# Gate rows written through DRAM by transfers, and half a gate tile ahead of the second attention pass's scores

## The chip, the core and the metric

The kernel runs on one core of one Trainium2 chip, as one launch. The metric is the time of one execution on the device in microseconds (us). It is the median of several runs; one more execution is profiled.

## The reference

Two transformer blocks in float32 over 256 tokens of width 1024. Cut to what matters here:

```
# first block
mod = silu(c) @ w_ada + b_ada;  shift_m, scale_m, gate_m, shift_f, scale_f, gate_f = split(mod, 6)
p = modulate(rms_norm(x), shift_m, scale_m) @ w_in
y_a = rwkv7_mix(p...)                 # recurrence over 12 heads, group norm, gate, @ w_a
y_b = dilated_attention_mix(p...)     # 12 heads in 3 groups, windows and dilations, @ w_b
x = x + gate_m * rms_norm((sigmoid(p_ga) * y_a + sigmoid(p_gb) * y_b) @ w_out)
x = x + gate_f * rms_norm(swiglu(modulate(rms_norm(x), shift_f, scale_f)))
# second block, for l in 0, 1
mod = (silu(c_2) @ w_ada[l] + b_ada[l]).reshape(3, 3, 1024)
x = x + 0.5 * mod[0, 2] * swiglu(ada_norm(x, 0))
x = x + mod[1, 2] * token_mixer(ada_norm(x, 1))
x = x + 0.5 * mod[2, 2] * swiglu(ada_norm(x, 2))
return rms_norm(x) * final_g
```

Every gate (`gate_m`, `gate_f`, `mod[., 2]`) is one number per column of the width, the same for all tokens. So is `final_g`.

## The kernel before

One program per engine, written out by hand. The engines meet at semaphores. Every transfer is issued by SP, in the order of its program, and SP does each wait in that order too.

**How a gate row comes about.** The modulation is computed by VectorE as dot products, one output per partition, so a gate lies as a column: `mod_gate` is [128, 8], the width spread over partitions and 8 columns. The hand-over at the end of a stage needs it as a row, [128, 1024], with the same 1024 numbers on all partitions (`row`). `gate_row` (L799) makes it on TensorE: 8 transposes, each of one column broadcast to [128, 128], into PSUM banks 2 and 3 (L804). `to_row` (L1501) copies the two banks to `row` on ScalarE (L1503). VectorE waits for `row_ready` and then multiplies the projection's banks by `row` (`quarter`, L1993 and L1995). There are nine such rows: n = 0 for the output projection of the first block, 1 for its FFN, 2 to 7 for the two layers (FFN, mixer, FFN each), and 8 for `final_g`.

**Where they stand.** Row 0 is made in the group norm at the end of `rwkv`, ahead of gate tiles 9 to 15. In `mixer2` the transposes stand behind the four native tiles of the first chunk (L1321). Row 8 is made at the very end: ScalarE copies it after its last square root (`norm`, L1605), and VectorE then scales both halves of the output with it (L2522, L2524), each half followed by a transfer out (L777).

**An FFN.** `ffn_split` exists once per engine. The hidden width is cut in 11 chunks (FC). Chunk 0 is multiplied natively, in two blocks of 64 matmuls, one per half of the tokens (L822), and `row_of()` runs the gate row behind them. From chunk 1 on, each weight is split in a high and a low part: ScalarE makes the high part (L1510 for up, L1518 for down), VectorE the low part (L1935, L1957), and TensorE does three matmuls for each product (L850 to L852, L866 to L868). TensorE's order is up(0), up(1), down(0), up(2), down(1) and so on. The up weights lie in two slots (`ring`, 2 MB a chunk), so SP loads those of chunk 2 when chunk 0's blocks are done (`half_done`), and then goes on in `step`: up weights, down weights, and in the first four FFNs four modulation weights of 512 KB.

**The merge.** `merge` (L1271) multiplies attention and recurrence outputs with `w_b` and `w_a` in 16 tiles, and VectorE and GpSimd combine them. Between the tiles VectorE does the late modulation products, one `late_row` load of 512 KB each (L718, four buffers). SP's order there is: w_b, side half of w_out, late rows 20 and 21, w_a in two loads, late rows 22 to 25, the positions (L750), the first half of w_out into the ring, late rows 26 to 31. `project` (L1005) is the output projection and needs both halves of w_out.

**Attention of the first block.** Four passes of three heads. `qk(i)` are pass i's scores (L1027, L1028), VectorE takes the maxima (L2104), ScalarE the exponentials (L1663), GpSimd scales them (L2597), TensorE turns them (L1051), VectorE copies them (L2134), and the products with v follow (L1063). `early_gate(j)` puts gate tiles of the first block's sigmoid gates between (L918): a tile is 8 accumulated matmuls over 256 tokens, which are 16 instructions in the profile. Before `qk(1)`, which waits for the first maxima, stands the selection of the head norms (L1038).

## Time and profile before

| | us |
|---|---|
| median of 3 runs | 1695.8 |
| lowest, highest | 1694.45, 1697.83 |
| the profiled execution, its own time | 1695.68 |
| its span, first to last instruction | 1693.9 |
| TensorE busy | 1619.6 (96% of the span) |
| VectorE busy | 1087.4 (64%) |
| ScalarE busy | 674.7 (40%) |
| mean granted TensorE clock | 0.994 |

The span is the time between the first and the last instruction of the profiled execution; 1.8 us lie around it. Busy times of one engine can be large without bounding anything; the chain of waits tells which work the end follows from. In all lines PE is TensorE, PEld its weight loads, DVE VectorE, ACT ScalarE, POOL GpSimd, SPq the issuing of transfers by SP, and L12 is line 12 of the kernel.

### The profile page before, as it was taken

How to read it: one execution, taken by the hardware profiler on the slowest of the kernel's cores; microseconds unless marked ns; L12 is line 12 of the kernel's file. 1: busy time of each engine (PE TensorE's matmuls, PEld its weight loads, DVE VectorE, ACT ScalarE, POOL GpSimd, SP SyncE). 2: the span in 40 equal slices, each digit the busy share in tenths (PEclk: the TensorE clock that was granted, in tenths of full speed). 3: DMA queues.
4: the chain of work that ended last, by engine and by line, in shares of the span. 5: the costliest groups of instructions: out<-in, count | busy, mean ns of one | idle time of the engine just before them, and what ended most of it. 6: DMA issues, size and time to landing. Idle time of an engine off the chain costs nothing.

```text
span 1693.9 us, 31871 instructions
## 1 busy us (share of the span) xinstructions
PE 1619.6 (96%) x13130; PEld 1440.8 (85%) x13130; DVE 1087.4 (64%) x1763; ACT 674.7 (40%) x1003; POOL 228.9 (14%) x292
## 2 busy tenths in 40 slices
PE   3999988898999989999999999999999999999997
PEld 3998778785999989999896699999999888589997
DVE  5985455464677757787656467776878666454544
ACT  3443433402433353333446433335333355543333
POOL 0431345131300000000015000000000012300000
PEclk9999999999999999999999999999999999999999
DMA  9853110285778728876540488765787542154540
GB/s 390 345 226 125 50 52 4 70 296 203 287 289 325 313 81 327 311 301 244 211 166 2 160 325 326 293 265 218 294 331 286 229 189 95 55 224 162 210 160 39
DMA packets 49928, 359.15 MB, mean 212 GB/s; under 512 B 5536, under 2 KB 6304, under 8 KB 29856
## 3 DMA queue, kind: packets, MB, share of 16 engines
q1 hardware_dynamic: 49824, 357.68, 55.1%
q8 instruction: 76, 1.25, 0.3%
q14 instruction: 28, 0.23, 0.0%
HBM read 356.61 MB, written 1.05 MB: 211 GB/s over the span
## 4 chain that ended last, share of the span: by engine, by line
PE 87%; DVE 5%; issue 3%; DMA 2%; POOL 1%; ACT 1%; SPq 0%; POOLq 0%; ACTq 0%; DVEq 0%
PE psum L852 11%; PE psum L851 11%; PE psum L850 11%; PE psum L866 5%; PE psum L867 5%; PE psum L868 5%; PE psum L1005 4%; PE psum L822 4%; PE psum L918 3%; PE psum L1271 2%; PE psum L954 2%; PE psum L955 2%; PE psum L956 2%; DMA arena<-in_ada_head 2%; PE psum L1291 1%
## 5 line engine op out<-in xcount | busy, mean ns | idle before, releaser
L850 PE MATMUL psum<-split 128*128 128x256 f32 x1600 | 453.0, 283 | 0.0
L852 PE MATMUL psum<-split 128*128 128x256 f32 x1600 | 452.8, 283 | 0.0
L851 PE MATMUL psum<-split 128*128 128x256 f32 x1600 | 452.8, 283 | 0.0
L850 PEld LDWEIGHTS psum<-split 128*128 128x128 f32 x1600 | 307.0, 192 | 1.8
L851 PEld LDWEIGHTS psum<-split 128*128 128x128 f32 x1600 | 307.0, 192 | 1.7
L852 PEld LDWEIGHTS psum<-split 128*128 128x128 f32 x1600 | 307.0, 192 | 0.0
L1935 DVE TENSOR_TENSOR split<-ring,split 128x2048 fp32r<-128x2048 f32 x100 | 228.6, 2290 | 58.4 <-ACT split L1510 53.6
L1510 ACT ACTIVATE split<-ring 128x2048 fp32r<-128x2048 f32 x100 | 190.6, 1911 | 177.6 <-PE psum L852 149.4
L1957 DVE TENSOR_TENSOR split<-ring_down,split 128x2048 fp32r<-128x2048 f32 x55 | 126.0, 2291 | 122.8 <-ACT split L1518 122.8
L1904 DVE CUSTOM_DVE_ANT_0 arena<-arena,c_row 128x1024 f32<-128x1024 f32 x144 | 167.6, 1220 | 0.0
L1518 ACT ACTIVATE split<-ring_down 128x2048 fp32r<-128x2048 f32 x55 | 105.3, 1915 | 136.6 <-PE psum L868 136.6
L2555 POOL TENSOR_TENSOR x_res<-x_res,scratch 128x512 f32<-128x512 f32 x16 | 20.5, 1279 | 1021.9 <-DVE scratch L1995 815.6
L866 PE MATMUL psum<-split 128*128 128x512 f32 x400 | 156.3, 391 | 0.0
L867 PE MATMUL psum<-split 128*128 128x512 f32 x400 | 156.2, 391 | 0.0
L868 PE MATMUL psum<-split 128*128 128x512 f32 x400 | 155.7, 389 | 0.0
L1529 ACT ACTIVATE scratch<-psum 128x512 f32<-128x512 f32 x55 | 33.0, 599 | 221.1 <-PE psum L852 212.1
L868 PEld LDWEIGHTS psum<-split 128*128 128x128 f32 x400 | 75.1, 188 | 16.1
L866 PEld LDWEIGHTS psum<-split 128*128 128x128 f32 x400 | 75.3, 188 | 14.4
L867 PEld LDWEIGHTS psum<-split 128*128 128x128 f32 x400 | 75.3, 188 | 13.8
L822 PEld LDWEIGHTS psum<-hT,ring 128*128 128x128 f32 x640 | 74.0, 195 | 6.8 <-issue 5.0
L822 PE MATMUL psum<-hT,ring 128*128 128x128 f32 x640 | 74.9, 279 | 4.8 <-DVE hT L2016 4.8
L1946 DVE TENSOR_TENSOR scratch<-scratch,psum 128x512 f32<-128x512 f32 x55 | 37.8, 687 | 61.2 <-ACT scratch L1529 61.1
(440 smaller groups left out, 2946.2 us busy)
## 6 DMA issues: line engine op xcount, KB each, us to landing
ring<-in_up SPq DMA_DIRECT2D x55, 2048.0 KB, 10.3
arena<-in_ada SPq DMA_DIRECT2D x168, 512.0 KB, 6.4
ring_down<-in_down SPq DMA_DIRECT2D x55, 1024.0 KB, 4.9
ring<-in_in SPq DMA_DIRECT2D x19, 2048.0 KB, 8.5
ring<-in_gates SPq DMA_DIRECT2D x4, 2048.0 KB, 8.6
arena<-in_ada_head SPq DMA_DIRECT2D x4, 1536.0 KB, 18.6
ring_down<-in_w_out SPq DMA_DIRECT2D x3, 2048.0 KB, 12.1
ring<-in_w_out SPq DMA_DIRECT2D x3, 2048.0 KB, 8.7
```

Of the source, the lines that this page charges most:

```text
L822: last = mm(dst, w[:, k * 512 + j * P:k * 512 + j * P + P], hT[:, k, t * P:(t + 1) * P], start=(t == 0 and k == 0 and j % 2 == 0), stop=(k ...
L850: mm(dst, up_hi[:, h, a], h_hi[:, kt_], start=(kt_ == 0 and j % 2 == 0), stop=False, skip_group_check=True)
L851: mm(dst, up_hi[:, h, a], h_lo[:, kt_], start=False, stop=False, skip_group_check=True)
L852: last = mm(dst, up_lo[:, h, a], h_hi[:, kt_], start=False, stop=(kt_ == KD - 1), skip_group_check=True)
L866: mm(bank[2 * t + h], act_hi[:, c % 2, a], dn_hi[:, w], start=(c == 0 and k == 0), stop=False, skip_group_check=True)
L867: mm(bank[2 * t + h], act_hi[:, c % 2, a], dn_lo[:, w], start=False, stop=False, skip_group_check=True)
L868: last = mm(bank[2 * t + h], act_lo[:, c % 2, a], dn_hi[:, w], start=False, stop=False, skip_group_check=True)
L1510: F(up_hi[:, h], ring[:, (g + c) % 2, h * 2048:(h + 1) * 2048], ACT.Copy).then_inc(up_high, 1)
L1518: F(up_hi[:, 1] if c == FC - 1 else dn_hi, ring_down[:, c % 2], ACT.Copy).then_inc(dn_high, 1)
L1904: return dve.tensor_tensor_reduce(out=weights, in0=weights, in1=c_of, scale=1.0, scalar=0.0, op0=ALU.mult, op1=ALU.add, accum_out=out)
L1935: tt(up_lo[:, h], ring[:, (g + c) % 2, h * 2048:(h + 1) * 2048], up_hi[:, h].bitcast(F32), ALU.subtract).then_inc(up_low, 1)
L1957: tt(d_lo, ring_down[:, c % 2], d_hi.bitcast(F32), ALU.subtract).then_inc(dn_low, 1)
```

## The change

TensorE's `gate_row` and ScalarE's `to_row` go, with all nine uses. In their place SP issues two transfers for each row: `row_out` writes the column (1024 elements of 4 bytes) to a row of a DRAM tensor, and `row_in` reads that row back to all 128 partitions of `row`, once it is written (`row_written`) and the row before it has been used (`fin_read`). VectorE's waits on `row_ready` count in steps of 16.

In an FFN the column goes out behind the loads of the first two down weights, and the row comes in when chunk 0's blocks are done, ahead of chunk 2's up weights. In a mixer the column goes out behind the compression weights and the row comes in behind the third weight chunk. Row 0's column goes out behind w_a and its row comes in behind late row 25, ahead of the positions and of w_out. The final row's column goes out in the last FFN, behind that FFN's own row; its row is loaded to `c2_row` at that FFN's end, and VectorE's last product reads it there.

Where TensorE waited for `row_ready` it now waits for `fin_read` in the FFN and for nothing elsewhere. Apart from this, `early_gate` and `tile` take a range of terms: the first four of gate tile 0's eight terms now run before `qk(1)`, the other four after it.

```diff
@@ -315,6 +315,7 @@
         c2_row = sb("c2_row", [P, D])
+        gate_rows = nc.dram_tensor("gate_rows", (9, D), F32, kind="Internal").ap()
         sums = sb("ada_sums", [P, 2, 4])
...
@@ -666,7 +667,17 @@
-            def ffn_split(g, f, done=None):
+            def row_out(n, column):
+
+                sp.dma_start(gate_rows[n].rearrange("(k p) -> p k", p=P), column, allow_slow_non_contiguous=True).then_inc(row_written, 16)
+
+            def row_in(n):
+
+                wait(sp, fin_read, 4 * n)
+                sp.wait_ge(row_written, 16 * (n + 1))
+                sp.dma_start(row[:], gate_rows[n:n + 1].broadcast_to([P, D])).then_inc(row_ready, 16)
+
+            def ffn_split(g, f, n, column, mods, done=None):
@@ -688,11 +699,20 @@
                     sp.dma_start(ring_down[:, c], T["down"][FC * f + c]).then_inc(down_full[c], 16)
+                sp.wait_ge(mod_ready, mods)
+                row_out(n, column)
                 sp.wait_ge(half_done, 2 * FC * f + 2)
+                row_in(n)
+                if f == ADA_FFNS:
+                    row_out(8, PR("final_g"))
                 with sp.Fori(0, FC - 3, 2) as i:
...
                 step(FC - 1)
+                if f == ADA_FFNS:
+                    sp.wait_ge(apart_used, 32 + 4 * ADA_PER_FFN * ADA_FFNS)
+                    sp.wait_ge(row_written, 16 * 9)
+                    sp.dma_start(c2_row[:], gate_rows[8:9].broadcast_to([P, D])).then_inc(s_c, 16)
                 released[:] = [(up_low, up_count(f, FC - 2)), (up_low, up_count(f, FC - 1))]
@@ -744,17 +764,21 @@
                 load(g + 5 + c, T["w_a"][c], (ym_full, 8 + 4 * (c + 1)))
+            sp.wait_ge(gn_dve, 1)
+            row_out(0, mod_gate[:, 0])
             for r in range(22, 26):
                 late_row(r)
+            sp.wait_ge(cm_evac, CM_G + 9)
+            row_in(0)
             sp.wait_ge(gn_pool, 2)
...
                 late_row(r)
-            ffn_split(G_FFN1, 0, DONE_MIX1 + 4)
+            ffn_split(G_FFN1, 0, 1, mod_gate[:, 1], 2, DONE_MIX1 + 4)
             for l in range(LAYERS):
                 g = G_LAYER + PER_LAYER * l
-                ffn_split(g, 1 + 2 * l)
+                ffn_split(g, 1 + 2 * l, 2 + 3 * l, mod_gate[:, 0], 3 + 2 * l)
                 g += FC
@@ -765,12 +789,16 @@
                         sp.dma_start(cmp_side, T["cmp1"][2 * l]).then_inc(cmp_loaded, 16)
+                        sp.wait_ge(mod_ready, 4 + 2 * l)
+                        row_out(3 + 3 * l, mod_gate[:, 1])
+                    if c == 2:
+                        row_in(3 + 3 * l)
                 sp.wait_ge(cmp_full, l + 1)
...
                 sp.dma_start(now[:], T["layers"][l + 1]).then_inc(s_layers, 16)
-                ffn_split(g + MIX2_CHUNKS, 2 + 2 * l, DONE_MIX2 + PER_LAYER_DONE * l + 4)
+                ffn_split(g + MIX2_CHUNKS, 2 + 2 * l, 4 + 3 * l, mod_gate[:, 2], 4 + 2 * l, DONE_MIX2 + PER_LAYER_DONE * l + 4)
             sp.wait_ge(s_layers, 16 * (LAYERS + 1))
@@ -796,20 +824,11 @@
-            def gate_row(n, column, part=range(KD)):
-
-                if part[0] == 0:
-                    wait(pe, fin_read, 4 * n)
-                for k in part:
-                    last = pe.transpose(bank[2 + k // 4][:, (k % 4) * P:(k % 4 + 1) * P], column[:, k:k + 1].broadcast_to([P, P]), ident)
-                if part[-1] == KD - 1:
-                    last.then_inc(row_full, 1)
-
...
-            def ffn_split(f, n, g, row_of):
+            def ffn_split(f, n, g):
@@ -830,7 +849,6 @@
                     block(1, w).then_inc(half_done, 2)
-                    row_of()
@@ -900,7 +918,7 @@
                 up(1)
-                pe.wait_ge(row_ready, n + 1)
+                pe.wait_ge(fin_read, 4 * n)
                 down(0)
@@ -910,14 +928,16 @@
-            def tile(table, base, j, w, dst=None):
-
-                wait(pe, cm_evac, since(base, j - 1))
+            def tile(table, base, j, w, dst=None, terms=range(KD)):
+
+                if 0 in terms:
+                    wait(pe, cm_evac, since(base, j - 1))
...
-                for k in range(KD):
+                for k in terms:
...
-                last.then_inc(cm_full, 1)
+                if KD - 1 in terms:
+                    last.then_inc(cm_full, 1)
@@ -1007,13 +1027,14 @@
-            def early_gate(j):
-
-                if j % 4 == 0:
-                    early_gate.w = chunk(G_GATES + j // 4)
-                if j != 1:
-                    pe.wait_ge(cm_evac, CM_G + j)
-                tile(TG, CM_G, j, early_gate.w, bank[3 if j == 1 else 0][:, 0:S])
+            def early_gate(j, terms=range(KD)):
+
+                if 0 in terms:
+                    if j % 4 == 0:
+                        early_gate.w = chunk(G_GATES + j // 4)
+                    if j != 1:
+                        pe.wait_ge(cm_evac, CM_G + j)
+                tile(TG, CM_G, j, early_gate.w, bank[3 if j == 1 else 0][:, 0:S], terms)
@@ -1037,8 +1058,9 @@
                 last.then_inc(kn_full, 1)
+                early_gate(0, range(4))
                 qk(1)
-                early_gate(0)
+                early_gate(0, range(4, KD))
                 early_gate(1)
@@ -1246,7 +1268,6 @@
                 last.then_inc(gn_sums, 1)
-                gate_row(0, mod_gate[:, 0])
                 pe.wait_ge(gn_dve, 2)
@@ -1324,8 +1345,6 @@
                             rotate(T2, base, rbase, 0)
-                pe.wait_ge(mod_ready, 4 + 2 * l)
-                gate_row(n, mod_gate[:, 1])
                 pe.wait_ge(cm_out, qbase + 1)
@@ -1340,8 +1359,6 @@
                     token_piece(p, IN2_WIDTHS[5], 6)
-                pe.wait_ge(row_ready, n + 1)
-
                 pe.wait_ge(side_loaded, 16 * (2 * l + 2))
@@ -1478,17 +1495,13 @@
-            pe.wait_ge(row_ready, 1)
...
-            pe.wait_ge(mod_ready, 2)
-            ffn_split(0, 1, G_FFN1, lambda: gate_row(1, mod_gate[:, 1]))
+            ffn_split(0, 1, G_FFN1)
...
-                pe.wait_ge(mod_ready, 3 + 2 * l)
-                ffn_split(1 + 2 * l, 2 + 3 * l, g, lambda: gate_row(2 + 3 * l, mod_gate[:, 0]))
+                ffn_split(1 + 2 * l, 2 + 3 * l, g)
...
-                ffn_split(2 + 2 * l, 4 + 3 * l, g + FC + MIX2_CHUNKS, lambda: gate_row(4 + 3 * l, mod_gate[:, 2]))
-            gate_row(8, PR("final_g"))
+                ffn_split(2 + 2 * l, 4 + 3 * l, g + FC + MIX2_CHUNKS)
@@ -1497,10 +1510,6 @@
-
-            def to_row(n):
-                act.wait_ge(row_full, n + 1)
-                f(row[:], psum[:, 2:4, :].rearrange("p b n -> p (b n)"), ACT.Copy).then_inc(row_ready, 1)
...
@@ -1529,8 +1538,6 @@
                         high_up(f, g, c + 1, 1, i)
-                    if c == 0:
-                        to_row(n)
                     high_down(f, c, i)
...
@@ -1868,14 +1872,12 @@
-            act.wait_ge(cm_evac, CM_G + 9)
-            to_row(0)
...
-            ffn_split(0, G_FFN1, 1)
+            ffn_split(0, G_FFN1)
...
@@ -2051,7 +2053,7 @@
-                dve.wait_ge(row_ready, n + 1)
+                dve.wait_ge(row_ready, 16 * (n + 1))
                 for j in range(3):
@@ -2516,12 +2518,12 @@
                     hand_over_last(4 + 3 * l, DONE_B + PER_LAYER_DONE * l, FC * (3 + 2 * l))
-            dve.wait_ge(row_ready, 9)
+            dve.wait_ge(s_c, 64)
             for t in range(NT):
...
                 v.settle()
-                stt(xn[:, t], x[:, t], stat[:, 6 + t:7 + t], row[:], ALU.mult, ALU.mult).then_inc(y_ready, 1)
+                stt(xn[:, t], x[:, t], stat[:, 6 + t:7 + t], c2_row[:], ALU.mult, ALU.mult).then_inc(y_ready, 1)
...
```

## Rows read from the trace of the kernel before

**Rows 1.** The page's part 4: the chain that ended last, shares of the span by engine

```profile
PE 87%; DVE 5%; issue 3%; DMA 2%; POOL 1%; ACT 1%; SPq 0%; POOLq 0%; ACTq 0%; DVEq 0%
```

**Rows 2.** Instructions by line, whole span: duration ns min/median/max, first and last start us

```profile
L804 PE MATMUL psum<-const,mod_gate x64: 272/273/273, 325.1 to 1508.3; 128*128 128x128 f32 x64
...
L1503 ACT ACTIVATE row<-psum x9: 1002/1026/1030, 328.5 to 1686.9; 128x1024 f32<-128x1024 f32 x9
```

**Rows 3.** The chain in order of time: start us, us, what; first and last FFN

```profile
430.15 0.87 PE psum L804 x8
...
1507.74 0.87 PE psum L804 x8
```

**Rows 4.** Timeline, TensorE, first mixer: start us, us, engine, line, op, idle before and releaser

```profile
826.04 1.13 PE L1332 MATMUL psum<-arena,const 128*128 128x256 f32 x4 [0.68 <-DVE arena L2096]
```

**Rows 5.** Timeline, TensorE, group norm of the first block

```profile
327.10 5.23 PE L918 MATMUL psum<-hT,ring 128*128 128x256 f32 x23 [0.98 <-DVE arena L2250]
```

**Rows 6.** Timeline, all engines, the tail of the kernel

```profile
1683.95 0.29 ACT L1601 ACTIVATE stat<-stat 128x1 f32<-128x1 f32 x1 [1.74 <-DVE stat L1973]
...
1685.94 0.15 DVE L1973 TENSOR_SCALAR stat<-stat 128x1 f32<-128x1 f32 x1
...
1687.97 0.16 DVE L2522 RECIPROCAL stat<-stat 128x1 f32<-128x1 f32 x1 [1.88 <-ACT row L1503]
...
1689.56 1.28 DVE L2524 SCALAR_TENSOR_TENSOR xn<-x_res,stat,row 128x1024 f32<-128x1024 f32 x1
```

**Rows 7.** Timeline, TensorE, attention of the first block

```profile
152.89 1.13 PE L1038 MATMUL psum<-xn,ring_down 32*128 32x512 f32 x6
...
155.20 0.79 PE L1027 MATMUL psum<-arena 64*128 64x128 f32 x2 [1.18 <-DVE neg_max L2118]
...
159.34 8.43 PE L918 MATMUL psum<-hT,ring 128*128 128x256 f32 x32
...
167.61 1.15 PE L1051 MATMUL psum<-const,arena 128*128 128x128 f32 x9
...
180.08 3.62 PE L918 MATMUL psum<-hT,ring 128*128 128x256 f32 x16
```

**Rows 8.** Windows: stretch, us, busy us of each engine, granted clock (PEclk), DMA share, GB/s

```profile
core 0: us, PE busy (x) PEld busy (x) DVE busy (x) ACT busy (x) POOL busy (x), PEclk, DMA share, GB/s
157.00:158.00 1.00, 1.00 (x5) 0.81 (x4) 0.01 (x1) 0.00 (x0) 0.89 (x1) 0.50 0.00 0
...
621.00:622.00 1.00, 1.00 (x7) 1.00 (x6) 0.15 (x1) 0.76 (x1) 0.00 (x0) 0.50 0.00 0
```

**Rows 9.** The chain in order of time, attention of the first block

```profile
169.78 3.43 POOL arena L2597 x2
```

**Rows 10.** DMA issues, whole span: KB each, median us from issue to landing

```profile
ring<-in_w_out SPq DMA_DIRECT2D x3, 2048.0 KB, 8.7
...
ring<-in_w_a SPq DMA_DIRECT2D x2, 1536.0 KB, 6.3
...
ring<-in_w_b SPq DMA_DIRECT2D x1, 1024.0 KB, 4.7
```

**Rows 11.** DMA queues and issues of the stretch 325 to 330 us

```profile
q1 hardware_dynamic: 144, 0.20, 14.7%
...
layer_now<-in_layers SPq DMA_DIRECT2D x1, 194.0 KB, 2.4
```

**Rows 12.** Timeline, VectorE, third and last FFN: splitting the third up weights

```profile
982.95 2.29 DVE L1935 TENSOR_TENSOR split<-ring,split 128x2048 fp32r<-128x2048 f32 x1 [5.01 <-ACT split L1510]
...
1518.32 2.29 DVE L1935 TENSOR_TENSOR split<-ring,split 128x2048 fp32r<-128x2048 f32 x1 [4.52 <-ACT split L1510]
```

**Rows 13.** Timeline, TensorE, third and last FFN: chunk 2's first matmul

```profile
989.58 0.28 PE L850 MATMUL psum<-split 128*128 128x256 f32 x1
...
1525.42 0.28 PE L850 MATMUL psum<-split 128*128 128x256 f32 x1
```

**Rows 14.** The chain in order of time, end of the merge

```profile
379.98 2.13 issue
```

**Rows 15.** DMA issues of the stretch 365 to 383 us

```profile
ring<-in_w_out SPq DMA_DIRECT2D x1, 2048.0 KB, 12.4
```

More of the change, by code:

```diff
@@ L466, in build @@
         ht_late = sem("ht_late")
-        row_full = sem("row_full")
+        row_written = sem("row_written")
         row_ready = sem("row_ready")
@@ L1518, in high_down, with ffn_split @@
                 F(up_hi[:, 1] if c == FC - 1 else dn_hi, ring_down[:, c % 2], ACT.Copy).then_inc(dn_high, 1)
-            def ffn_split(f, g, n):
+            def ffn_split(f, g):
                 def one(c, i=0):
@@ L1603, in norm @@
                     first_modulated()
-                    return
-                to_row(n)
             def high_piece(j):
@@ L1788, in mixer2 @@
                     high_piece2(j - 1)
-                to_row(n)
                 for p in range(3, 7):
@@ L1885, in _ @@
                     norm_halves(2 + 3 * l, 0, 3 + 2 * l)
-                ffn_split(1 + 2 * l, G_A, 2 + 3 * l)
+                ffn_split(1 + 2 * l, G_A)
                 norm_halves(3 + 3 * l, 1, 4 + 2 * l, split=False)
@@ L1889, in _ @@
                 norm_halves(4 + 3 * l, 2, 4 + 2 * l)
-                ffn_split(2 + 2 * l, G_B, 4 + 3 * l)
+                ffn_split(2 + 2 * l, G_B)
             norm(8)
@@ L2052, in hand_over_last @@
             def hand_over_last(n, done, downs):
-                dve.wait_ge(row_ready, n + 1)
+                dve.wait_ge(row_ready, 16 * (n + 1))
                 for j in range(3):
```

## The prediction

> **What bounds the kernel now.** I read the chain that ended last first. TensorE carries 87% of it [rows 1], so an edit counts only where it takes time off TensorE's own queue, fills a gap in it, or moves what TensorE waits for. Then I read the nine gate rows (the instructions by line, and where the chain passes over them), then the timelines of the places that the diff touches: the second attention pass, the merge, the first chunks of an FFN, and the last twenty microseconds. Last come SP's issues and the transfers, since all that the change adds is put there.
>
> **Gate rows on TensorE and ScalarE, removed.** A gate row is 8 transposes on TensorE and one copy of about 1.0 us on ScalarE [rows 2]. In each of the five FFNs the transposes stand between the first chunk's half blocks and chunk 1, and the chain runs over them at 0.87 us; the first and the last are shown [rows 3]. What chunk 1 needs first is ready by then, so it moves up by the whole: 5 x 0.87 = **4.35 us**. The copy on ScalarE runs beside chunk 1's matmuls, so it is worth nothing there. In both mixers TensorE sits idle right after the gate row until VectorE's rope result is there [rows 4]: without the transposes it is only idle for longer, 0. The first gate row, in the group norm, likewise ends in a wait for VectorE [rows 5], 0. The ninth is in the tail.
>
> **The tail.** VectorE's two output products start only when ScalarE has copied the row, at 1687.97, although the root of the first half is there from 1684.24 on and VectorE is free from 1686.09 [rows 6]. After: reciprocal and product at once (0.16 + 1.28 us), so the first product ends near 1687.6 and the second near 1689.06 instead of 1689.56 + 1.28 = 1690.84. That is **1.78 us**; the second output transfer then sets the end, as now. The final row's own transfers are issued at the start and at the end of the last FFN, ahead of all this.
>
> **Half a gate tile ahead of the second pass's scores.** TensorE ends the head selection at about 153.9 and sits idle 1.18 us until VectorE has the first maxima at 155.15 [rows 7]. What follows is slow: the second scores take 155.20 to 159.34, and two gate tiles (32 instructions) 8.43 us where one takes 3.62 at 180.08. The granted clock there is 0.50, the lower of the two levels, 1.2 GHz [rows 8]. Before it fell, TensorE had run small matmuls and then nothing. With 8 instructions (half a tile, 1.8 us) in the gap it runs on from 153.9 to 155.7. If the clock then stays at 2.4 GHz, the scores take half of 4.14 = 2.07 and end at 157.7, the remaining 24 instructions take 5.4, and the transposes begin at 163.1 instead of 167.61: **4.5 us**. What they wait for, the exponentials and the scaling of pass 0, began right behind the first maxima and is done by then. Next on the chain come VectorE's copies and, behind them, GpSimd's scaling of pass 1 [rows 9]; it waits for the reciprocal that VectorE does after these copies, so it moves by as much. If the clock falls all the same, only the idle 1.18 us is gained. I take 4.5: TensorE is idle for 2.13 us later and the clock is not seen to fall, and here no gap would be left.
>
> **Transfers added: the row in.** Each gate row is now 512 KB written to all partitions. 1536 KB land in 6.3 us and 1024 KB in 4.7 [rows 10], so 512 KB more take 1.6 us of the engines; I take that.
>
> **Transfers added: the column out.** 1024 elements of 4 bytes each, to rows in DRAM. No row of this kernel shows such a transfer. Below: nothing beside its issue, some 0.4 us. Above: 128 packets of 1.5 KB held 14.7% of 16 engines for 5 us, which is 92 ns each [rows 11]; at 64 packets an engine that is 5.9 us. A far end takes its whole 2.4 us to landing per 128 packets, and so 19 us for 1024. I take 2 us, nearer to the lower end, since most of those 2.4 us is latency that does not repeat per packet. The Trainium skill speaks against this form: the page DMA: Bandwidth & Descriptors (Rules for kernel authors) has a strided last dimension become one descriptor per element and advises against it. Its one price for tiny packets (Bandwidth, Measured), about 10.5 ns each, would make 0.7 us of 64, as an estimate, and the time 1686.9. No run here shows either.
>
> **Where these transfers stand in SP's queue.** In the five FFNs the column goes out right behind the two first down weights. SP then waits for the first chunk's half blocks, which come after TensorE's whole normalisation gap and 128 matmuls, so the column is hidden, its write receipt too. The row goes in directly ahead of the third up weights. SP issues those 0.33 + 1.6 = 1.9 us later. Their slack: in the third FFN (the tightest of the five) VectorE's split of them ends at 982.95 + 2.29 = 985.24, and TensorE wants them at 989.58, in future 0.87 earlier: 3.5 us. So there is no stall in the first four, though it becomes one if the row costs over 3.2 us. In the last FFN the slack is 1525.42 - 0.87 - (1518.32 + 2.29) = 3.9 us [rows 12, 13], but there the column of the final row stands in front too: 1.9 + 0.4 + 2 = 4.3, a stall of **0.4 us**. In the mixers the column follows the compression weights, while SP waits for the native tiles; the row follows a 2 MB load, and the next load waits for pieces that are still to be split: 0.
>
> The merge is the sore place. After its last tile TensorE waits 2.13 us, from 379.98 on [rows 14], with every operand from VectorE but the last ready: it waits for the output projection's weights. These take 12.4 us from issue to landing there [rows 15] against 8.7 in the median [rows 10]. So some 3.7 us of other transfers are queued ahead of them, and what is added to that queue comes out at TensorE. Added are one column (2 us) and one row (1.6 us), less some 0.5 us of gaps in the queue: **3.1 us** lost. VectorE's late modulation products behind it move as well, and so does the norm that wants them.
>
> **Added waits.** SP waits for the written column before each row comes in: at the merge at most 1 us, within the queue's 3.7. Queued behind it are the positions and the projection's weights, for which TensorE waits. VectorE's wait for the row comes at the end of each FFN, nine chunks behind the transfer.
>
> **Sum.** -4.35 - 1.78 - 4.5 + 3.1 + 0.4 = -7.1 us on the span of 1693.9. The profiled execution took 1695.68 us, which is 1.8 us around the span and in line with the median of 1695.8. So 1695.7 - 7.1 = **1688.6 us**.
>
> **Rivals.** (a) The clock falls in the attention pass all the same. For it: the stretch before it holds matmuls on a part of the array only, and the clock is at 0.50 in the second hand-over too [rows 8], so one gap need not be the whole cause. Against it: the gap is gone. Price 4.5 - 1.2 = 3.3 us: 1691.9. (b) Slower: the column out costs much more than 2 us. Each microsecond of it above that is paid twice, in the merge and in the last FFN. At 5.6 us the whole gain is gone; at 8 us the kernel takes 1688.6 + 12 = 1700.6. For it: 1024 tiny writes into one 4 KB row. Against it: the per-packet time of small packets here. (c) The projection's weights aren't pushed, since the queue has gaps enough, and the final column is cheap: 1688.6 - 3.5 = 1685.1. (d) The gate rows' time isn't freed, because the next operand is late or the row delays the third up weights more than I think: 1688.6 + 4.35 = 1692.9. Beside all these, moving everything by some microseconds can make or unmake a fall of the clock in a hand-over, about 1.7 us either way.
>
> **How the numbers follow.** Forecast 0.48 (its own range 1685.5 to 1692); (a) 0.15, (b) 0.19, (c) 0.13, (d) 0.05. About 0.2%, 3.4 us, is what a measurement can tell from no change, so the borders are 1692.4 and 1699.2. Faster: nearly all of the forecast and (c), a little over half of (a), half of (d), say 0.69. Slower: the part of (b) with a column over 7.3 us, 0.13. The rest, 0.18, is the same. The range of 8 in 10 runs from 1683.5 to 1698: it takes in (a), (c), (d) and the part of (b) up to a column of 6.7 us, with the upper bound of 5.9 us inside.
>
> **What would show it.** No L804 or L1503 work, and chunk 1's first matmul 0.1 us behind the first chunk's last; granted clock 1.00 from 155 to 162 and the first transposes near 163; TensorE's gap after the merge 5 us instead of 2.1; in the last FFN a gap ahead of chunk 2 under 1 us; the two output products back to back. I'd be wrong if the column held the queue for over 5 us, if the clock fell to 0.5 near 155 again, or if the gap after the merge stayed at 2 us.

## The result

The changed kernel is slower. Kernels are compared by their ratio to the kernel before on the same chip:

| | kernel before | changed kernel |
|---|---|---|
| median, us | 1698.99 (1694.45 to 1701.59, 9 runs) | 1707.80 (1702.41 to 1711.79, 9 runs) |
| ratio to before, 95% interval | | 1.0051 (1.0035 to 1.0068) |
| the same in a later comparison (E13) | 1697.36 | 1702.13, 1.0024 (1.0014 to 1.0034) |
| profiled execution, us; its span | 1695.68; 1693.9 | 1704.6; 1702.8 |
| TensorE busy, us | 1619.6 | 1616.6 |

The forecast was 1688.6 us, faster. In the two profiled executions the changed kernel's span is 8.9 us longer. The page of the changed kernel, its part 4, then its small packets (part 2) and the issues of the new transfers (KB each, median us to landing):

```profile
PE 82%; DMA 7%; DVE 5%; issue 2%; ACT 2%; POOL 1%; SPq 0%; POOLq 0%; DVEq 0%; ACTq 0%
...
DMA packets 60584, 363.89 MB, mean 214 GB/s; under 512 B 15041, under 2 KB 15809, under 8 KB 40513
...
row<-gate_rows SPq DMA_DIRECT2D x8, 512.0 KB, 5.2
...
gate_rows<-mod_gate SPq DMA_DIRECT2D x8, 4.0 KB, 15.7
gate_rows<-params SPq DMA_DIRECT2D x1, 4.0 KB, 14.6
```

Transfers now carry 7% of the chain instead of 2% [rows 1]. The 4 KB of a column take 15.7 us to land in the median (13.9 to 19.9), three times as long as the 512 KB of a row.

**Where the time went.** Landmarks on TensorE's timeline: start in the kernel before, and how much later (+) or earlier (-) the others are. Clean is the kernel of experiment E7.

| landmark, us | before | changed | clean |
|---|---|---|---|
| transposes of the second pass | 167.61 | -4.36 | -2.59 |
| merge begins | 352.11 | -0.59 | -2.53 |
| output projection begins | 382.10 | +3.57 | -3.27 |
| first FFN: chunk 0 ends | 430.15 | +5.01 | -3.24 |
| first FFN: chunk 1 begins | 430.78 | +4.13 | -4.12 |
| third FFN: chunk 1 begins | 972.51 | +0.80 | -7.49 |
| third FFN: chunk 2 begins | 989.58 | +1.64 | -7.50 |
| last FFN: chunk 1 begins | 1508.37 | -0.16 | -9.37 |
| last FFN: chunk 2 begins | 1525.42 | +8.67 | -9.37 |
| last FFN: first matmul of the last down product ends | 1676.04 | +10.83 | -9.37 |
| end of the span | 1693.9 | +8.9 | -11.3 |

The last FFN alone loses 11 us. Chain of the changed kernel in order of time (start us, us, what), first the merge, then the third and the last FFN:

```profile
359.07 14.72 DMA gate_rows<-mod_gate
...
374.71 10.92 DMA ring<-in_w_out
```

```profile
959.32 15.37 DMA gate_rows<-mod_gate
...
975.44 11.46 DMA ring<-in_up
...
986.92 1.93 ACT split L1519
988.87 2.30 DVE split L1937
```

```profile
1494.21 15.05 DMA gate_rows<-mod_gate
...
1509.71 0.44 SPq L672
...
1510.51 19.28 DMA ring<-in_up
...
1529.81 1.92 ACT split L1519
1531.75 2.30 DVE split L1937
```

In all three SP sits at its wait for the written column, and the chain goes on over that wait into the load behind. In the last FFN the third up weights also queue behind the final row's column: 19.28 us to landing. TensorE, timeline of the changed kernel at the three places (start, duration, idle before and releaser), to hold against [rows 13, 14]:

```profile
385.68 1.22 PE L1025 MATMUL psum<-ring,arena 128*128 128x512 f32 x1 [4.32 <-DMA ring<-in_w_out]
...
991.22 0.39 PE L868 MATMUL psum<-split 128*128 128x256 f32 x1 [0.69 <-DVE split L1937]
...
1534.10 0.58 PE L868 MATMUL psum<-split 128*128 128x256 f32 x1 [8.67 <-DVE split L1937]
```

Part of the stall is paid twice, because the clock falls in it. Windows of the changed kernel, columns as in [rows 8]; the granted clock is the third number from the right:

```profile
1534.00:1538.00 4.00, 3.90 (x18) 3.91 (x19) 3.93 (x6) 1.80 (x1) 0.00 (x0) 0.50 0.15 61
...
1540.00:1542.00 2.00, 2.00 (x19) 2.00 (x18) 0.23 (x1) 0.00 (x0) 0.00 (x0) 1.00 0.59 66
```

From 1534.1 to 1538.8 TensorE works at 1.2 GHz, which costs 2.2 us more.

The merge loses in two ways. Waits of the changed kernel, 350 to 390 us (idle in total, times, longest):

```profile
DVE xn L1906 <- DMA xn<-in_ada: 9.9, 2, 5.1
...
PE psum L1292 <- DVE arena L2275: 1.7, 1, 1.7
```

VectorE waits 9.9 us for late rows, which are queued behind the column (2.9 us in the kernel before), and TensorE 1.71 us for VectorE inside the merge. Then come 4.32 us for the projection's weights, where the kernel before has 2.1.

**What a column does.** DMA of the changed kernel while the last FFN's column is out, issued at 1494.21 and landed at 1509.26. Packets of 1499 to 1501.5 us, then of 1501.5 to 1509:

```profile
DMA packets 1110, 0.45 MB, mean 182 GB/s; under 512 B 1056, under 2 KB 1056, under 8 KB 1056
...
DMA packets 0, 0.00 MB, mean 0 GB/s; under 512 B 0, under 2 KB 0, under 8 KB 0
```

Until then the down weights ahead of it move. The column's 1024 packets are over by 1501.5, in the trace's packet records 9 ns each. Then no packet runs for 7.5 us, and the column lands. The time is not in the packets. SP has issued nothing else in this stretch, so it does not show that other transfers are held up. The final row's column shows that: its packets run from 1513.2 to 1514.6, with three loads of weights (5 MB) queued behind it. Packets of 1515 to 1524 us:

```profile
DMA packets 34, 0.56 MB, mean 62 GB/s; under 512 B 0, under 2 KB 0, under 8 KB 0
```

In the packet records a 16 KB packet takes 0.61 us in the median. The 16 of the up weights that start between 1514.2 and 1515.2, behind the column's, take 4.9 to 9.2 us each. No other 16 KB packet of this execution takes over 4.5 us, and none of the clean kernel's over 2.7.

### The profile page after: what moved, and what is told of

Same layout as the page of the kernel before. It is cut to its first block, busy times and chain, and to the rows that moved or that the text cites. A ratio compares the mean times of both kernels' runs of the same rounds, so it can differ in the third digit from the quotient of the medians.

```text
span 1702.8 us, 31736 instructions
## 1 busy us (share of the span) xinstructions
PE 1616.6 (95%) x13058; PEld 1435.9 (84%) x13058; DVE 1087.5 (64%) x1763; ACT 665.5 (39%) x994; POOL 227.9 (13%) x292
## 4 chain that ended last, share of the span: by engine, by line
PE 82%; DMA 7%; DVE 5%; issue 2%; ACT 2%; POOL 1%; SPq 0%; POOLq 0%; DVEq 0%; ACTq 0%
PE psum L868 11%; PE psum L870 11%; PE psum L869 11%; PE psum L884 5%; PE psum L885 5%; PE psum L886 5%; PE psum L1025 4%; PE psum L937 3%; DMA gate_rows<-mod_gate 3%; PE psum L841 2%; DMA ring<-in_up 2%; DMA arena<-in_ada_head 2%; PE psum L974 1%; PE psum L975 1%; PE psum L976 1%
## 5 line engine op out<-in xcount | busy, mean ns | idle before, releaser
L885 PEld LDWEIGHTS psum<-split 128*128 128x128 f32 x400 | 75.3, 188 | 13.9
```

The costliest lines, as they stand in the source:

```text
L885: mm(bank[2 * t + h], act_hi[:, c % 2, a], dn_lo[:, w], start=False, stop=False, skip_group_check=True)
```

## Experiments

Theory C, formed on these rows: the column's many small writes hold up the queue and whoever waits. All ratios are to the kernel before on the same chip. A difference given in us is the ratio's, on some 1697 us, where the text doesn't say medians. E6 and E9 ran once each, for their traces.

| | kernel | median, us | ratio, 95% interval |
|---|---|---|---|
| E1 | before + half tile | 1691.71 | 0.9973 (0.9959 to 0.9988) |
| E2 | gate rows by transfers only | 1704.15 | 1.0047 (1.0029 to 1.0065) |
| E3 | changed, final column early | 1696.68 | 0.9993 (0.9980 to 1.0006) |
| E4 | E3 + row 0 early | 1695.44 | 0.9989 (0.9978 to 1.0000) |
| E5 | changed, packed columns | 1691.10 | 0.9964 (0.9952 to 0.9977) |
| E7 | clean | 1687.95 | 0.9950 (0.9936 to 0.9964) |
| E8 | before + tail | 1694.69 | 0.9990 (0.9978 to 1.0001) |
| E10 | clean + near column | 1693.34 | 0.9970 (0.9952 to 0.9987) |
| E11 | clean + far column | 1686.10 | 0.9925 (0.9908 to 0.9941) |
| E12 | clean + two columns early | 1695.79 | 0.9987 (0.9974 to 1.0000) |
| E13 | changed, again | 1702.13 | 1.0024 (1.0014 to 1.0034) |
| E14 | E2 again | 1706.48 | 1.0048 (1.0030 to 1.0066) |
| E15 | clean, whole gate tile | 1688.68 | 0.9955 (0.9940 to 0.9970) |
| E16 | clean, again | 1687.18 | 0.9936 (0.9918 to 0.9953) |

### E1 and E2: the two parts alone

E1 is the kernel before with the two lines below and the `terms` of the change's diff. E2 is the changed kernel with them undone.

```diff
+                early_gate(0, range(4))
                 qk(1)
-                early_gate(0)
+                early_gate(0, range(4, KD))
```

> The kernel before with half a gate tile ahead of the second pass's scores, and nothing else of the change. Theory H (the gain is handed back by the clock later): in the changed kernel the transposes of the second pass begin 4.4 us earlier, but the recurrence holds two stretches at half clock (3 us and 11 us) where the kernel before has one of 3.5 us, so that only 0.6 us is left at 326 us. Then this kernel takes 0.5 to 1 us less than before (1698.99 us), its trace has transposes near 163.2, a second stretch at 0.50 between 228 and 245, and the group norm's gate tiles near 327. Rival H2 (the half tile's gain lasts and the rest of the change ate it): 4.4 us less than before, no second stretch at 0.50, the gate tiles near 323.

> The changed kernel without the half gate tile: all gate rows by transfers. Theory C (each column of 1024 elements takes 15 us from issue to landing and holds what is queued behind it): the three losses are all here, so slower than before by 8 to 10 us, near 1708.5; merge and hand-over lose about 5.6 us, the last FFN about 11, the tail and the five FFNs gain about 6. Rival (the losses come from the earlier start that the half tile gives, which shifts the stages against the transfers): at most 3 us slower than before, near 1701.

E1: 0.9973, which is 4.6 us; its transposes begin at 162.91, 4.70 us sooner. Theory H, my first reading of the table above (0.6 us left at the merge), falls; the forecast's own term was right. E2: 1.0047, which is 8.0 us slower. So theory C has the sign and the size, and the loss is all in the transfers. Windows 155 to 162 us, E1, then E14 (as E2):

```profile
155.00:162.00 7.00, 7.00 (x35) 5.73 (x34) 3.96 (x18) 3.20 (x9) 3.44 (x2) 1.00 0.00 0
```

```profile
155.00:162.00 7.00, 5.82 (x23) 4.43 (x21) 5.25 (x28) 3.20 (x8) 3.44 (x2) 0.76 0.00 0
```

The clock is granted in full in every profiled kernel with the half tile (13 of them), and falls in all five without it. It does not fall as far in all five. The same window of the kernel before:

```profile
155.00:162.00 7.00, 6.80 (x19) 5.30 (x20) 4.09 (x19) 1.99 (x5) 3.44 (x2) 0.51 0.00 0
```

From the end of the head selection to the transposes it takes 13.58 us, at half clock for 6.8. In E2, E8, E14 and E15 it is at half clock for 3.4 us and takes 12.0, and with the half tile 9.30 in all 13. So the half tile is worth 4.3 us against the profile of the kernel before and 2.7 us against the other four.

### E3 and E4: columns moved to where nothing is queued

```diff
             for c in range(4):
                 load(g + c, T["gates1"][c], (cm_full, 32 + 4 * (c + 1)))
+            row_out(8, PR("final_g"))
...
-                if f == ADA_FFNS:
-                    row_out(8, PR("final_g"))
```

E4 has, besides:

```diff
+            sp.wait_ge(s1_max, 1)
+            row_out(0, mod_gate[:, 0])
...
             for r in (20, 21):
                 late_row(r)
+            sp.wait_ge(cm_evac, CM_G + 9)
+            row_in(0)
```

and not the two in the merge.

> The changed kernel with one column moved: that of the final row goes out behind the loads of the fourth gate chunk at about 215 us, where nothing is queued behind it for 100 us, instead of ahead of the third up weights in the last FFN. Theory C (the column itself holds up the third up weights): the stall of 8.7 us ahead of chunk 2 in the last FFN goes, and with it the 4.7 us at half clock behind it (2.3 us of work): 11.0 us less than the changed kernel (1707.8), near 1696.8; the third up weights land 9 to 11 us after their issue. Rival B (the bytes of the row that comes in at the same place, 0.5 MB, do it): the stall shrinks by 2 us at most, the time stays above 1704.

> As the kernel with the final column early, and row 0 taken out of the merge's queue as well: its column goes out at about 216 us, its row comes in behind late row 21 (near 345 us), so that neither stands ahead of the positions and the output projection's weights. Theory C (SP's wait for the written column, 5 us, delays the weights): the projection starts as long after the merge's last tile as before (2.1 us, not 4.3), the hand-over behind it is as before too, and about 5.6 us more are gained: near 1691.2 us, 7 to 8 us less than the kernel before. Rival Q (the merge loses because TensorE arrives earlier at a queue that is full of bytes anyway): at most 2 us more than the kernel with the final column early, near 1695.

E3 did what theory C says: no stall in the last FFN (chunk 1 to chunk 2 takes 17.06 us, before 17.06, changed 25.89). Its ratio is 0.0058 under the changed kernel's first, 10 us, and 0.0031 under its second (E13), 5 us; 11 were expected, and the trace of the last FFN shows 11. E4 is short of its forecast by 4 us. The merge is mended: from its first matmul to the end of chunk 0 it takes 79.56 us (before 78.04, changed 83.64). But the recurrence takes 108.53 us where before takes 97.54. No rival of mine was about that. VectorE's waits of E4 in 218 to 245 us, then the same of E7 (idle in total, times, longest):

```profile
DVE arena L2193 <- remote: 12.7, 2, 10.0
```

```profile
DVE arena L2202 <- PE psum L1186: 9.2, 4, 5.9
```

### E5 and E7: the same bytes in 128 runs of 32

```diff
+def by_partition(w):
+
+    w = np.array(w)
+    for at in range(2 * D, w.shape[-1], 3 * D):
+        w[..., at:at + D] = w[..., at:at + D].reshape(*w.shape[:-1], P, KD).swapaxes(-1, -2).reshape(*w.shape[:-1], D)
+    return w
...
+    for name in ("w_ada", "w_ada_2", "b_ada", "b_ada_2"):
+        g[name] = by_partition(g[name])
...
-                sp.dma_start(gate_rows[n].rearrange("(k p) -> p k", p=P), column, allow_slow_non_contiguous=True).then_inc(row_written, 16)
+                sp.dma_start(gate_rows[n].rearrange("(p k) -> p k", k=KD), column).then_inc(row_written, 16)
```

The scales and `final_g` are laid out alike. E7 adds row 0 as in E4 and the final row from a row of the inputs:

```diff
-                    sp.wait_ge(row_written, 16 * 9)
-                    sp.dma_start(c2_row[:], gate_rows[8:9].broadcast_to([P, D])).then_inc(s_c, 16)
+                    sp.dma_start(c2_row[:], T["final_row"].broadcast_to([P, D])).then_inc(s_c, 16)
```

> The changed kernel with the gate columns in another order: the weights and biases of the gates are laid out so that partition p holds the 8 neighbouring elements 8p to 8p+7, and a column goes out as 128 runs of 32 bytes instead of 1024 elements of 4 bytes. Same bytes, same waits, same places in the queue. Theory C (the number of small writes is what costs): a column lands 2 to 4 us after its issue instead of 15; the third up weights in the last FFN land about 9 to 10 us after their issue, the stall ahead of chunk 2 is under 1 us and no half clock follows it; the merge's stall is 2 to 3 us. About 11 + 3 us less than the changed kernel, 6 to 8 us less than before: ratio 0.996. Rival L (a small write that is waited for costs 10 us or more whatever its packets, or its place in the queue does): columns still take over 10 us and the time stays within 4 us of the changed kernel.

> As the kernel with packed columns, and with the final row read from a row of the inputs (no column for it) and row 0 moved: its column goes out at about 215 us, its row comes in behind late row 21, out of the merge's queue. Theory C with the sum of the prediction but without its transfer terms: 4.35 + 1.8 + about 4.5 less than before, -10.6: ratio 0.9938 of before. Theory F (loading of program code): the kernel with both columns early at 215 us lost 4 us more than expected, with VectorE idle for 10.00 us right behind them and TensorE waiting for nothing that the profile shows; by this, 128 runs there cost nothing and the recurrence from 221.9 to its group norm takes the 89 to 92 us of the other kernels, not 99.6. Rival (the recurrence loses for another reason, its start time): it stays near 99 and the ratio is 0.998 or more.

E5 settles that it is the column's form: same places, same waits, same bytes, and 0.9964 instead of 1.0051 and 1.0024 (E13). Rival L falls. No stall in the last FFN, 2.68 us behind the merge. Its columns land in 6.8 us in the median, most of which is the queue ahead. E7 goes further, to 0.9950; TensorE waits 1.38 us behind the merge, and the recurrence takes 97.59 us with a column in it. Of the 10.6 us expected 8.5 came; 10.9 in E16, 12.7 in E11 with its extra column. The clean kernel beats both kernels.

### E6 and E9: forms of a column, one at a time

```diff
+            probe(probe_half[0, 0:512].rearrange("(k p) -> p k", p=P), PR("final_g", 0, 4))
+            probe(probe_packed[0].rearrange("(p k) -> p k", k=KD), PR("final_g"))
+            probe(probe_far.rearrange("(k p) n -> p k n", p=P)[:, :, 0], PR("final_g"))
+            probe(now[:, 0:16:2], PR("final_g"))
+            probe(probe_line, c2_row[0:1])
```

> Five more transfers, one at a time, in the recurrence (from about 240 us on), none of which is used: 512 elements of 4 bytes to DRAM, 128 runs of 32 bytes to DRAM, 1024 elements of 4 bytes to DRAM 512 bytes apart, 1024 elements of 4 bytes to SBUF, one run of 4 KB to DRAM. Theory C, by elements: 15 us for 1024 elements, some 8 to 9 for 512, 2 to 4 for the 32-byte runs and for the single run. Theory C1 (the writes pile up at the memory, since their packets are over within 2 us while the landing comes 8 us later): the 1024 elements to SBUF land in 4 us or less, and those 512 bytes apart in DRAM sooner than 15 us if it is one place of the memory that is crowded, and in 15 again if each small write costs alike. Theory C2 (the engines' work per element): 15 us to SBUF too.

> The clean kernel with six unused columns of 1024 elements of 4 bytes in the recurrence, one at a time, to DRAM at distances of 128, 64, 32, 16, 8 and 4 bytes from element to element. From the forms tried before: 512 bytes apart took 2.5 us, adjacent ones 15 us. Theory A (small writes into the same short line of the memory wait for each other): 2.5 us for the far ones, then a rise where several elements share a line, up to 15 us at 4 bytes; if a line is 64 bytes, 128 and 64 take 2.5 and 32, 16, 8, 4 take more, each about as long as the number of elements to a line says, or the full time at once. Rival (the 15 us belong to the row of 4 KB as a whole, the total reach): a steady rise from 128 down to 4, with no step.

SP waits for each landing before it issues the next, so the distance of two issues is a form's time. SP's timeline of E6 (start, duration), single issues:

```profile
237.19 0.36 SPq L763 DMA_DIRECT2D probe_half<-params  x1
246.98 0.33 SPq L763 DMA_DIRECT2D probe_packed<-params  x1
248.39 0.36 SPq L763 DMA_DIRECT2D probe_far<-params  x1
250.93 0.71 SPq L763 DMA_DIRECT2D layer_now<-params  x1
253.31 0.31 SPq L763 DMA_DIRECT2D probe_line<-c_row  x1
```

512 adjacent elements take 9.8 us, 128 runs of 32 bytes 1.4, 1024 elements 512 bytes apart 2.5, 1024 to SBUF 2.4. So neither the count nor the engines' work per element costs (C2 falls, and so does C's reckoning by elements). What costs is small writes next to each other in DRAM. E9, the same for distances of 128, 64, 32, 16, 8 and 4 bytes:

```profile
224.79 0.38 SPq L770 DMA_DIRECT2D spare_by<-params  x1
...
227.82 0.37 SPq L770 DMA_DIRECT2D spare_by<-params  x1
...
230.63 0.36 SPq L770 DMA_DIRECT2D spare_by<-params  x1
...
233.53 0.36 SPq L770 DMA_DIRECT2D spare_by<-params  x1
...
237.17 0.36 SPq L770 DMA_DIRECT2D spare_by<-params  x1
...
241.29 0.36 SPq L770 DMA_DIRECT2D spare_by<-params  x1
```

The columns are spaced by `.rearrange("(k p n) -> p k n", p=P, n=step)[:, :, 0]`. That is 3.0, 2.8, 2.9, 3.6 and 4.1 us. The last, adjacent, has its landing records from 249.97 to 252.22: 10.9 us. There is a step, as theory A says, but between 8 bytes and 4, where A had it at the length of a line; its reason stays open. In the adjacent form neighbouring elements also come from neighbouring partitions; whether small adjacent writes out of one partition cost as much was not tried.

### E10 and E11: the cost put back

```diff
+                if f == ADA_FFNS:
+                    spaced = spare_out[0:D * 1].rearrange("(k p n) -> p k n", p=P, n=1)[:, :, 0]
+                    sp.dma_start(spaced, PR("final_g"), allow_slow_non_contiguous=True).then_inc(row_written, 16)
```

E11 has 128 in place of 1.

> The clean kernel (packed columns, 1687.95 us) with one unused column of 1024 adjacent elements of 4 bytes added ahead of the third up weights in the last FFN, where the changed kernel has that of the final row. Theory C: the stall of about 8.7 us ahead of chunk 2 comes back, and half clock behind it: 10.5 to 11 us more than the clean kernel, near 1698.7, ratio to before 1.001. Rival (it was the three transfers together, with the real row's wait): 5 us more at most.

> The same added column with its elements 512 bytes apart in DRAM: the same 1024 elements and bytes in the same place. Theory A (adjacency costs, not the count): it lands in about 3 us, third up weights a good 2 us late at most, within their slack of 3.9 us: no stall, within 1 us of the clean kernel, near 1688. Rival (the count of elements costs once other transfers are queued behind it): stall of 5 us or more, above 1694.

TensorE's waits of E10, 1495 to 1560 us; E11 has none there:

```profile
PE psum L880 <- DVE split L1949: 6.4, 1, 6.4
```

6.4 us of stall and 2.6 at half clock, 7.2 us between the medians of E10 and E11. That is a third less than the 10.5 expected, and more than the rival's 5. The wait for the real row's column isn't in it; in the changed kernel that column lands 0.8 us behind the chunk's end, so it explains only part. The far column costs nothing that four runs can show.

### E8 and E12: the tail, and columns in the recurrence

E8 is the kernel before with:

```diff
                 step(FC - 1)
+                if f == ADA_FFNS:
+                    sp.wait_ge(apart_used, 32 + 4 * ADA_PER_FFN * ADA_FFNS)
+                    sp.dma_start(c2_row[:], T["final_row"].broadcast_to([P, D])).then_inc(s_c, 16)
...
-            gate_row(8, PR("final_g"))
```

without its copy on ScalarE, and VectorE's last product reads `c2_row`. E12 is the clean kernel with two unused adjacent columns behind its own at 215 us:

```diff
             row_out(0, mod_gate[:, 0])
+            for spare in (spare_one, spare_two):
+                sp.dma_start(spare[0:D].rearrange("(k p) -> p k", p=P), PR("final_g"), allow_slow_non_contiguous=True).then_inc(probed, 16)
```

> The kernel before with the final row loaded to a free buffer from a row of the inputs in the last FFN, instead of being turned by TensorE and copied by ScalarE at the end. Nothing else. Theory T: VectorE's two output products follow their roots at once, 1.78 us less than before: ratio 0.9990, at the edge of what can be measured; in the trace the first product ends about 1.78 us sooner behind the last FFN's end. Rival: the second root or the transfer out sets the end, 0.3 us or less.

> The clean kernel with two unused columns of 1024 adjacent elements added behind its own column at about 215 us, in the recurrence, where no transfer of data is queued behind them for 100 us. Theory F (the engines' program code comes through the same transfer engines and waits behind the columns): VectorE and TensorE idle for 5 to 10 us at about 222 to 235 with nothing in the profile that they wait for, the recurrence takes 95 to 100 us instead of 88.7, ratio to before about 0.999 instead of 0.995. Rival (the loss in the kernel with both columns early was the clock's alone): the recurrence grows only by what its stretches at half clock explain, no idle time of VectorE near 10 us.

E8: from the last down product's first matmul to the end 15.9 us instead of 17.86, 1.97 us in the trace, and a ratio of 0.9990 that alone can't be told from 1. E12: the recurrence takes 107.90 us instead of 97.59. VectorE's idle time that no engine releases is there as in E4:

```profile
DVE arena L2206 <- remote: 12.3, 2, 8.7
```

Not all of the 10 us is this. The recurrence (from TensorE's matmul at 226.26 in before, to the second sums of the group norm) in the profiled executions, by how long the clock was at 0.50 in it:

| us at half clock | recurrence takes, us |
|---|---|
| 3.4 | 97.54 (before), 97.59 (E7), 97.60 (E11) |
| 6.8 | 98.45 (E1), 98.42 (E2), 98.48 (E15) |
| 13.7 | 101.30 (changed), 100.63 (E13), 101.11 (E5), 101.20 (E16) |
| 17 | 102.24 (E8), 102.30 (E10), 102.27 (E14) |
| 20.5 | 102.87 (E3), 107.90 (E12), 108.53 (E4) |

The time at half clock differs between executions of one kernel (3.4 in E7 and 13.7 in E16, 6.8 in E2 and 17 in E14). The column of E3, issued at 215.4 us and landed at 229.05, costs nothing beyond the clock; two cost 5 to 6 us more. It is not the number: in E9 the one adjacent column is out from 241.29 to 252.22, and the recurrence takes 108.23 us at 20.5 us of half clock. VectorE, timeline of E9:

```profile
252.28 0.29 DVE L2209 TENSOR_TENSOR arena<-arena,psum 128x128 f32<-128x128 f32 x1 [6.27 <-remote]
```

This instruction reads nothing of that column, and TensorE's matmuls that it waits for ended at 247.8. It starts 0.06 us behind the column's landing, and TensorE's next matmul has waited 5.92 us for it. In E6 two idle stretches of VectorE end in the same way, at 237.35 and 247.09, 0.17 and 0.12 us behind the landings at 237.18 and 246.97. So a column can hold up VectorE where no data waits for it. Beside the columns, the transfer engines carry little but program code there (16 KB at a time on the queue named instruction, 0.31 MB from 226 to 314 us in the kernel before). That the code waits behind the columns is the likely reason, but was argued, not isolated.

### E13 to E16: do the parts add up?

E15 is E7 with the whole gate tile behind `qk(1)`; the others are kernels named above.

> The changed kernel, unaltered, beside its parts on one chip. Theory S (the parts add up; the difference of 5 us is the intervals'): 3 to 5 us slower than before, ratio about 1.0025. Rival X (the half tile's gain is lost where the columns are): 8 to 9 us slower, ratio 1.005, no better than the kernel with the gate rows by transfers alone.

> Gate rows by transfers and the whole gate tile behind the second scores, beside the changed kernel. Theory S: 4.5 us slower than the changed kernel. Rival X: within 1 us of it.

> The clean kernel without the half tile: packed columns, final row from the inputs, row 0 out of the merge's queue, the whole gate tile behind the second scores. If the half tile is worth 4.6 us here as in the kernel before: ratio 0.9975, 4 to 5 us slower than the clean kernel; its trace has half clock from about 155 to 162 again. Rival: within 1.5 us of the clean kernel, which would say that the recurrence's own stretches at half clock take the gain back.

> The clean kernel beside these. Both theories: ratio to before 0.9935 to 0.9955, as its two measurements so far (0.9950, and 0.9925 with an unused spaced column).

In the changed kernel they do: 1.0048 without and 1.0024 with the half tile, 4.1 us apart (S), and rival X falls. In the clean kernel it is 3.2 us by the ratios (0.9955, 0.9936) and 1.5 us by the medians, under the 4 to 5 expected; the intervals overlap, so the rival's 1.5 us is not excluded there. The changed kernel is slower by 0.24% here and by 0.51% in the first comparison; that spread stays unexplained.

## Why the prediction failed

**Gate rows on TensorE, -4.35: right.** From the end of chunk 0 to chunk 1 each of the five FFNs gains 0.87 to 0.88 us.

**The tail, -1.78: right**; 1.9 us in the changed kernel, 1.97 in E8.

**The half gate tile, -4.5: right in mechanism, the size in part luck.** The clock no longer falls at 155 us. The transposes come 4.36 us sooner, and the ratios give 4.6 and 4.1 us (E1, E14 against E13). But the fall that the sum removed was the deep one of the profile before; against the four other profiles without the half tile it is worth 2.7 us in place. The changed kernel's own trace seems to deny it, -0.59 at the merge. The table by half clock explains that: its recurrence drew 13.7 us at 1.2 GHz, the kernel before's 3.4, and E8, almost the kernel before, 17.

**The column out, 2 us: here it failed.** It takes 15. My bounds were built on time per packet, and that is 9 ns. The Trainium skill (DMA: Bandwidth & Descriptors, Bandwidth, Measured) has about 10.5 ns for loads to SBUF issued from GpSimd, and the trace's 9 ns are near it; but the 0.7 us made from that price as an estimate was the furthest off. What I set aside was nearer: the advice of the Trainium skill (the same page, Rules for kernel authors) to make the last dimension contiguous, which with the packed column took the loss away, and my far end of 19 us. That one is near by luck: it multiplied the landing time of another transfer by eight, and the time lies behind the packets, in their landing.

**"The column is hidden" in the FFNs, its write receipt too: false in the third, fourth and last.** In the third and the last the columns went out at 959.32 and 1494.21, 14.2 us ahead of the first chunk's end, and landed after 15.37 and 15.05; in the fourth the column landed 1.3 us behind the chunk's end, without a stall. Third FFN: 0.69 us of stall, which takes the row's gain back (E13's execution has none there). The slack of 3.5 us [rows 12, 13] was right; it was used up by SP's wait, the row and a slower landing.

**The merge, +3.1: right sign, 5.6 lost** by the end of chunk 0 (1.9 in the merge's own tiles, 2.3 ahead of the projection, 1.4 at half clock from 385 us). The queue's bytes hardly did it: with packed columns (E5) the same bytes cost 0.6 us, a stall of 2.68 instead of 2.13, and nothing in the tiles (1.7 us more at half clock follow). Two things did it. The added wait was priced "at most 1 us"; SP stood 5 us at it, and issued the projection's weights at 374.71 instead of 369.65 (369.80 with packed columns). And the late rows behind the column came late for VectorE, which the prediction mentions and prices at nothing.

**The last FFN, +0.4: 11 us**, 8.67 of stall and 2.2 at half clock.

**Rival (b)** is what happened, mechanism and places. At 15 us its rule of two for one would give 1714.6, which is too much: part of the landing passes while SP waits anyway. Half clock was not in it. Its chance, 0.19, and an example that ends at 8 us came from trusting the packet's time. (a) and (c) didn't happen, (d) only as the 0.69 us of the third FFN.

**The sum**, with the column's cost removed, comes near, in part by luck: -10.6 was left of it, and the clean kernel measured 8.5 to 10.9 less than before. Two misses about cancel. The half tile is mostly worth 1.8 us less than 4.5, as said. And from chunk 1 of the first FFN to that of the second, the profile of before takes 200.0 us, as E1 and E8 do, and 14 of the 15 profiled kernels with rows by transfers 197.5. Of these 2.5 us the gate row is 0.87; the other 1.64 are chunk 0's second half at half clock, from 619.3 us on in the kernel before, which they don't have there. The prediction named such a shift beside the sum ("about 1.7 us either way") and did not count it.

## What to carry to other kernels

A tiny transfer is priced by its time to landing and by what stands still meanwhile, not by its bytes or packets: if no row shows its form, measure one in a quiet place before building on it. Write a column out in runs, and let the layout of the weights put neighbours on one partition. Before an added wait on a receipt, list what is queued behind the waiting engine, and compare its slack with the whole landing time, not with the issue.

## What was new about the hardware

1024 writes of 4 bytes to adjacent places of DRAM took 10.9 us alone and 13.9 to 19.9 us in the changed kernel, with other transfers ahead. At 8 bytes' distance they took 4.1 us, at 32 to 512 bytes' 2.5 to 3.0, to SBUF 2.4, and 128 runs of 32 bytes 1.4, with packets of about 9 ns in all of them (one execution each, E6 and E9). The 16 KB packets that started behind adjacent ones took 4.9 to 9.2 us instead of 0.61. And the same stretch of the recurrence was at half clock for 3.4 to 20.5 us from one profiled execution to the next, worth up to 5 us, which is why one trace of each kernel could not tell what became of the half tile.
